# One core, 1 x 256 tokens: the gates of the first 128 tokens go through device memory by adding indirect DMAs, in both expert layers

## The chip, the cores and the metric

One core of one Trainium2 chip runs the whole program. The metric is device microseconds from start to end, lower is better. PE is the matrix engine (TensorE), DVE the vector engine (VectorE), ACT the scalar engine (ScalarE), POOL is GpSimd, and SP is the queue that issues most DMAs.

## The reference, cut to what matters

The reference is a block of two layers on 256 tokens of width 1024 (an attention-like mix, then an expert layer), followed by another block with its own attention and MLP. The change touches only the expert layer, which is computed twice (layer 0 and layer 1). Each has 16384 experts; an expert is one row of `u` and one row of `v`. Each of 8 heads chooses 16 experts per token, so a token has 128 (expert, gate) pairs, and the same expert may be chosen by more than one head:

```python
def block(args):
    ht, et, gt = args                       # tokens, their experts, their gates
    act = jax.nn.gelu(jnp.einsum('td,ted->te', ht, u[et]), approximate=False)
    return jnp.einsum('te,ted->td', gt * act, v[et])
```

## The kernel before

The expert layer (`peer`, L1282) does not gather. It computes the activation of every expert for every token and multiplies by a dense matrix of gates, which is zero where an expert is not chosen.

**First pass, U.** For j = 0 to 127, TensorE multiplies 128 experts' rows (U[j]) by all 256 tokens, GELU is applied, and the result lies in `av[:, j, 0:256]`: partition p and column j stand for expert 128 p + j. Each weight tile of 512 KB is split by ACT (`hi`) and DVE (`lo`) into two parts, two tiles ahead at most, and multiplied in three products (hi by hi, hi by lo, lo by hi). SP loads the raw tiles into a ring of four, each after `lo` of the tile four before it. From j = 80 to 125 (`PAIRED`) the hi products of both halves of the tokens' matrix run as one of 512 columns, and ACT and DVE add them together.

**Choices.** Meanwhile DVE works through `choices` (L1494), tile t = 0 (first 128 tokens) and then t = 1: the 16 greatest of each side, their sums, the greatest 16 of those, the experts' numbers (`EF`), then the exponentials on ACT (L1388) and the normalised gates (`GT`). A sum of costs (`COST`) spreads this over the steps up to j = 74.

**Products of one-hots.** At j = 76 and 77 PE transposes the experts' upper and lower numbers and the gates (`E1`, `E2`, `GT`), so that column n belongs to token n. From step `C_FROM` = 78 on, 64 groups of four tokens are worked off: for a token n, `oneA` holds the gate where iota equals the upper number, `oneB` is 1 where iota equals the lower, and PE multiplies the two, 128x128, which gives the token's gates for all 16384 experts in PSUM. POOL builds two of the four `oneA` of a group (L1353), ACT one or two in two steps (`hots_ac`, L1451), DVE the rest and `oneB` of all four (`hots`, L1572). A group may be built when the group two before it has been multiplied ("prod"). Groups are laid on steps by `GROUPS`; after group g, ACT copies the gates of later experts into `av` (L1405), DVE multiplies the earlier ones in place, and GELU results of the tokens done so far (`AHEAD`) go through `gtmp` and `gate_tile` (L1584). The one-hots lie in the memory of x, which is saved to `xs` in device memory ahead of the pass and read back in the second.

**Second pass, V.** For j = 0 to 127, ACT and DVE split `av[:, j, :]` (`coef_high`, L1466, `coef_low`, L1477) and the tile V[j], and PE adds twelve products of 512 columns into four banks. In layer 0 the same ring of four also carries 48 tiles of another weight (`ada`), which DVE multiplies on (`modulation_ve`, L1635).

Of the kernel before, what the change touches and what calls it, by code (L numbers as in the profile page):

```python
# [41 lines left out]
for _name, _w in [("ident", 128), ("ones", 128), ("bd64", 128), ("ntri", 128), ("nones", 128), ("sbm", 128), ("flip", 128),  # L42
                  ("fmask", 384), ("gm", 7 * 64), ("reset", 256), ("hot", 384), ("iota", 128), ("negrow", 8),
                  ("cneg", 2 * 16), ("cok", 2 * 16)]:
    CST[_name] = (_n, _n + _w)
    _n += _w
# [12 lines left out]
def constants():  # L59
# [40 lines left out]
    put("cneg", np.where(ok > 0, 0.0, NEG))  # L100
    return c
# [4 lines left out]
for _sem, _events in (  # L106
# [5 lines left out]
        ("cmp_pe", "cmp hidT kvc kc_ss lc PcTp")):  # L112
# [39 lines left out]
class Engine:  # L152
# [74 lines left out]

    def dma_start(self, out, in_):
        return Done(self, self.e and self.e.dma_start(out, in_), 16)
# [46 lines left out]
def declare(nc, arrays):  # L276
# [9 lines left out]
    io["xs"] = nc.dram_tensor("xs", (128, 2048), F32, kind="Internal").ap()  # L286
    return io
# [7 lines left out]
def build(nc, io, ctx):  # L295
# [967 lines left out]
    eT = [cbuf[:, 256 * i:256 * i + 256] for i in range(5)]  # L1263
# [8 lines left out]
    AFTER = [C_FROM + g * (C_TO - C_FROM) // 64 for g in range(64)]  # L1272
    GROUPS = [[g for g in range(64) if AFTER[g] == j] for j in range(128)]
    AHEAD = [4 * sum(AFTER[g] < j for g in range(64)) for j in range(128)]

# [6 lines left out]
    def peer(layer):  # L1282
# [21 lines left out]
        V = [table("v", 0)]  # L1304
        for j in range(128):
            if j < 127:
                V.append(table("v", j + 1))
            if layer == 0 and 4 <= j < 124 and (j - 4) % 2 == 0 and (j - 4) % 10 < 8:
# [12 lines left out]
        def peer_sp(sp):  # L1321
# [11 lines left out]
            sp.dma_start(io["xs"], xTf[:, :]).then_inc("x_out", layer)  # L1333
            for i, (src, freed, _) in enumerate(tiles):
                if i == 140:
                    sp.wait_ge("prod", layer, 63)
# [5 lines left out]
        gain = lambda c: P(f"f{layer}", c)  # L1342

        OWN = (0, 1, 2, 4, 5, 6)

        def peer_po(po):
            norm_po(po, k, gain)
            po.wait_ge("x_out", layer)
            for g in range(64):
                s = 4 * (g % 2)  # L1350
                po.wait_ge("eT", layer, g // 32)
                if g >= 2:
                    po.wait_ge("prod", layer, g - 2)  # L1353
                for i in range(2):
                    n = 4 * g + i
                    d = po.tensor_scalar(oneA[:, s + i, :], iota, eT[0][:, n:n + 1], EQ, eT[2][:, n:n + 1], MUL)
                d.then_inc("hotP", layer, g)

        def peer_ac(ac):
# [23 lines left out]
            for j in range(128):  # L1383
# [7 lines left out]
                if j in (C_FROM - 1, C_FROM):  # L1391
                    t = j - C_FROM + 1
                    ac.wait_ge("eTp", layer, t)
                    w = slice(128 * t, 128 * t + 128)
                    for i in range(3):
                        ac.activation(eT[i][:, w], PS[:, 4 + t, 128 * i:128 * i + 128], COPY)
                    for i in range(2):
                        d = ac.activation(eT[3 + i][:, w], PS[:, 4 + t, 128 * i:128 * i + 128], COPY, scale=-1.0)
                    d.then_inc("eT", layer, t)
                    if t == 0:  # L1400
                        ac.wait_ge("x_out", layer)
                        hots_ac(ac, 0)
                        hots_ac(ac, 1)
                for g in GROUPS[j - 1] if j else []:
                    ac.wait_ge("prod", layer, g)  # L1405
                    ac.activation(av[:, j:128, 4 * g:4 * g + 4], PS[:, 4 + g % 4, :].rearrange("p (t j) -> p j t", t=4)[:, j:128, :],
                                  COPY).then_inc("placed", layer, g)
                    if g < 62:
# [8 lines left out]
                elif j >= J_LATE:  # L1417
                    ac.wait_ge("eT", layer, 1)
# [22 lines left out]
        def gelu(ac, j, src):  # L1441
            n = AHEAD[j]
            if n:
                if j >= C_FROM + 3:
                    ac.wait_ge("gated", layer, "tile", j - 2)
                d = ac.activation(gtmp[:, j % 2, 0:n], src[:, 0:n], ACT.Gelu)
            if n < 256:
                d = ac.activation(av[:, j, n:256], src[:, n:256], ACT.Gelu)
            d.then_inc("gelu", layer, j)

        def hots_ac(ac, g):  # L1451
            s = 4 * (g % 2)
            ac.wait_ge("eT", layer, g // 32)
            for i in (2, 3) if g % 4 == 1 else (2,):
                n, a = 4 * g + i, oneA[:, s + i, :]
# [10 lines left out]
        def coef_high(ac, j):  # L1466
            if j >= 3:
                ac.wait_ge("wdone", V[j - 3])
            if j == 0:
                ac.wait_ge("hotP", layer, 63)  # L1470
                ac.wait_ge("hot", layer, 63)
                ac.wait_ge("gated", layer, 63)
# [21 lines left out]
        def choices(ve):  # L1494

            g, s = GT.rearrange("p (h k) -> p h k", h=16), SC.rearrange("p (h k) -> p h k", h=16)
            for t in range(2):
# [31 lines left out]
                if t:  # L1529
                    ve.tensor_tensor(g, s, s[:, :, 0:1].broadcast_to([128, 16, 16]), SUB).then_inc("gmax", layer)  # L1530
                hv = hot.rearrange("p (k c) -> p k c", k=16)
                for h in range(8):
# [10 lines left out]
                    yield 10  # L1543
            ve.wait_ge(*d)
            ve.wait_ge(*ve.tensor_copy(EI, EF).then_inc("dveC"))
            ve.tensor_scalar(E2.bitcast(U32), EI, 127, ALU.bitwise_and)
            ve.wait_ge(*ve.tensor_scalar(E1.bitcast(U32), EI, 7, ALU.logical_shift_right).then_inc("dveC"))
            ve.tensor_copy(E2, E2.bitcast(U32))
            ve.tensor_copy(E1, E1.bitcast(U32)).then_inc("e12", layer)
            yield 15  # L1550
            ve.wait_ge("gexp", layer)
            ve.wait_ge(*ve.tensor_reduce(st[:, 0:16], g, ADD).then_inc("dveC"))
            ve.wait_ge(*ve.reciprocal(st[:, 16:32], st[:, 0:16]).then_inc("dveC"))
            ve.tensor_tensor(g, g, st[:, 16:32].rearrange("p (h o) -> p h o", o=1).broadcast_to([128, 16, 16]), MUL).then_inc("gates", layer)
            yield 10

        COST = 2 * (16 * 15 + 6 + 28 + 8 * 13 + 8 * 30) + 25

        def peer_ve(ve):
# [12 lines left out]
            def hots(g):  # L1572
# [3 lines left out]
                ve.wait_ge("eT", layer, g // 32)  # L1576
                n = 4 * g + 3
                if g % 4 != 1:
                    ve.tensor_scalar(oneA[:, s + 3, :], iota, eT[0][:, n:n + 1], EQ, eT[2][:, n:n + 1], MUL)
                ve.tensor_tensor(oneB[:, s:s + 4, :], iota.rearrange("p (o e) -> p o e", o=1).broadcast_to([128, 4, 128]),  # L1580
                                 eT[1][:, 4 * g:4 * g + 4].rearrange("p (t o) -> p t o", o=1).broadcast_to([128, 4, 128]),
                                 EQ).then_inc("hot", layer, g)

            def gate_tile(j):  # L1584
                n = AHEAD[j]
                if n:
                    ve.wait_ge("gelu", layer, j)
                    ve.tensor_tensor(av[:, j, 0:n], av[:, j, 0:n], gtmp[:, j % 2, 0:n], MUL).then_inc("gated", layer, "tile", j)

            for j in range(128):  # L1590
                if j == C_FROM:
                    ve.wait_ge("x_out", layer)
                    hots(0)
# [7 lines left out]
                for g in GROUPS[j - 1] if j else []:  # L1601
                    ve.wait_ge("placed", layer, g)
                    ve.wait_ge("gelu", layer, j - 1)
                    m = av[:, 0:j, 4 * g:4 * g + 4]
                    ve.tensor_tensor(m, m, PS[:, 4 + g % 4, :].rearrange("p (t j) -> p j t", t=4)[:, 0:j, :], MUL).then_inc("gated", layer, g)
                    if g < 62:
# [81 lines left out]
        def peer_pe(pe):  # L1688
# [1431 lines left out]
```

## Time and profile before

| | us |
|---|---|
| median of 3 runs | 2362.92 |
| lowest, highest | 2362.66, 2363.53 |
| profiled execution, first to last instruction | 2361.0 |
| PE busy | 2335.1 (99%) |
| DVE busy | 1755.3 (74%) |
| ACT busy | 1367.7 (58%) |
| POOL busy | 463.4 (20%) |
| DMA, share of 16 engines | 54.6% |

The times of the rows are microseconds, where nothing else is said, and stand for one execution. A busy engine is one with an instruction in flight; PE's products overlap, so the distance between two starts says more than a duration. "x16" is a count, "<-" names what an idle engine waited for, and L170 and the like are lines of helpers, so that tiles and shapes tell the places apart.

### The profile page before, as it was taken

The page shows a single profiled execution, that of the slowest core. Times are in us where ns is not written, and L with a number is a line of the kernel's source. Part 1 is how long each engine was busy: PE and PEld are TensorE (multiplying, and loading weights), DVE is VectorE, ACT ScalarE, POOL GpSimd, SP SyncE. Part 2 cuts the span into 40 slices and gives each one's busy share as a digit, 9 for nine tenths or more (in the row PEclk, how much of TensorE's full clock was granted, in tenths as well). Part 3 has the DMA queues.
Part 4 walks back from the last instruction along what each step waited for, and adds up shares of the span by engine and source line. Part 5 has one row for each costly group of instructions (what it writes and reads, how often), then busy time and mean ns, then how long its engine had stood idle before and what let it go on. Part 6 is the DMA issues. An engine that isn't in the chain of part 4 may idle for free.

```text
span 2361.0 us, 40110 instructions
## 1 busy us (share of the span) xinstructions
PE 2335.1 (99%) x15655; PEld 2115.9 (90%) x15655; DVE 1755.3 (74%) x3335; ACT 1367.7 (58%) x2622; POOL 463.4 (20%) x411
## 2 busy tenths in 40 slices
PE   8999999999999999999999999999999999999999
PEld 8899999999888888888999999998888888899998
DVE  7967999788777777667599988885555555747864
ACT  6664445777655555566544467775554454666643
POOL 4720000788300000011000038870000000003000
PEclk9999999999999999999999999999999999999999
DMA  7234565444588888732266654446666675334452
GB/s 279 88 131 127 181 187 178 148 131 134 186 269 263 270 262 269 281 144 109 94 187 184 181 172 132 134 134 205 194 192 194 195 234 200 140 113 174 179 193 75
DMA packets 93283, 421.77 MB, mean 179 GB/s; under 512 B 10324, under 2 KB 12956, under 8 KB 85160
## 3 DMA queue, kind: packets, MB, share of 16 engines
q1 hardware_dynamic: 92784, 418.84, 54.6%
q8 instruction: 126, 2.06, 0.4%
q14 instruction: 61, 0.50, 0.1%
q10 hardware_dynamic: 312, 0.37, 0.0%
HBM read 415.98 MB, written 3.18 MB: 178 GB/s over the span
## 4 chain that ended last, share of the span: by engine, by line
PE 91%; DVE 6%; ACT 2%; DMA 1%; issue 1%; ACTq 0%; DVEq 0%
PE PS L170 90%; DVE r_sl L191 2%; DVE mem L191 1%; DVE mem L199 1%; ACT mem L181 1%; ACT r_sh L181 1%; DMA mem<-in_v 1%; PE PS L173 0%; DVE mem L205 0%; DVE mem L211 0%; DMA cst<-in_cst 0%; DVE r_gl L199 0%; DVE hT L199 0%; ACT L188 0%; DVE mem L195 0%
## 5 line engine op out<-in xcount | busy, mean ns | idle before, releaser
L191 DVE TENSOR_TENSOR r_sl<-mem,r_sh 128x1024 fp32r<-128x1024 f32 (+2 forms) x750 | 896.4, 1196 | 452.8 <-ACT r_sh L181 450.8
L181 ACT ACTIVATE r_sh<-mem 128x1024 fp32r<-128x1024 f32 (+2 forms) x750 | 767.5, 1024 | 493.9 <-PE PS L170 408.0
L170 PE MATMUL PS<-r_h,r_sh 128*128 128x256 f32 (+2 forms) x4800 | 752.6, 304 | 6.3 <-ACT r_h L181 2.8
L170 PEld LDWEIGHTS PS<-r_h,r_sh 128*128 128x128 f32 (+1 forms) x4800 | 647.5, 191 | 42.5 <-issue 8.9
L196 POOL TENSOR_SCALAR xT<-cst,mem 128x128 f32<-128x128 f32 x256 | 328.3, 1294 | 543.4 <-ACT mem L181 492.9
L170 PE MATMUL PS<-r_h,r_sl 128*128 128x256 f32 (+1 forms) x2832 | 400.7, 283 | 1.2 <-DVE r_sl L191 1.1
L170 PEld LDWEIGHTS PS<-r_h,r_sl 128*128 128x128 f32 (+1 forms) x2832 | 371.7, 191 | 10.9 <-DVE r_sl L191 2.2
L181 ACT ACTIVATE mem<-PS 128x256 f32<-128x256 f32 (+19 forms) x468 | 158.9, 351 | 324.1 <-PE PS L170 322.5
L170 PE MATMUL PS<-r_sh,r_ch 128*128 128x512 f32 x1024 | 276.1, 390 | 2.2 <-ACT r_sh L181 2.2
L170 PE MATMUL PS<-r_sh,r_cl 128*128 128x512 f32 x1024 | 274.8, 389 | 0.0
L170 PE MATMUL PS<-r_sl,r_ch 128*128 128x512 f32 x1024 | 274.7, 389 | 0.0
L170 PEld LDWEIGHTS PS<-r_sh,r_ch 128*128 128x128 f32 x1024 | 191.2, 188 | 47.0 <-ACT r_sh L181 4.9
L170 PEld LDWEIGHTS PS<-r_sh,r_cl 128*128 128x128 f32 x1024 | 192.2, 188 | 40.1
L170 PEld LDWEIGHTS PS<-r_sl,r_ch 128*128 128x128 f32 x1024 | 192.2, 188 | 40.0
L170 PE MATMUL PS<-xT 128*128 128x128 f32 x1024 | 130.0, 275 | 0.0
L170 PEld LDWEIGHTS PS<-xT 128*128 128x128 f32 x1024 | 122.8, 192 | 0.0
L191 DVE TENSOR_TENSOR r_cl<-mem,r_ch 128x256 fp32r<-128x256 f32 x256 | 106.9, 418 | 11.3 <-ACT r_ch L181 11.3
L181 ACT ACTIVATE r_ch<-mem 128x256 fp32r<-128x256 f32 x256 | 102.4, 400 | 3.9 <-issue 3.9
L181 ACT ACTIVATE mem<-mem 128x256 f32<-128x256 f32 (+5 forms) x153 | 79.8, 531 | 32.4 <-DVE mem L205 23.6
L170 PE MATMUL PS<-mem 64*15 64x64 f32 (+9 forms) x1014 | 96.4, 289 | 2.1 <-ACT mem L181 1.0
L170 PEld LDWEIGHTS PS<-mem 64*128 64x128 f32 (+4 forms) x1014 | 79.4, 153 | 20.9 <-issue 9.0
L181 ACT ACTIVATE small<-PS 128x256 f32<-128x256 f32 (+2 forms) x108 | 42.9, 398 | 78.3 <-PE PS L170 78.1
(170 smaller groups left out, 2504.4 us busy)
## 6 DMA issues: line engine op xcount, KB each, us to landing
mem<-in_u SPq DMA_DIRECT2D x256, 512.0 KB, 3.6
mem<-in_v SPq DMA_DIRECT2D x256, 512.0 KB, 4.4
mem<-in_w SPq DMA_DIRECT2D x16, 2048.0 KB, 8.2
mem<-in_ada SPq DMA_DIRECT2D x48, 512.0 KB, 4.9
mem<-in_in SPq DMA_DIRECT2D x9, 2048.0 KB, 8.8
mem<-in_wq SPq DMA_DIRECT2D x8, 2048.0 KB, 7.7
mem<-in_od_in SPq DMA_DIRECT2D x6, 2048.0 KB, 9.7
mem<-in_ev_in SPq DMA_DIRECT2D x5, 2048.0 KB, 14.4
```

What stands on the lines that cost most here:

```text
L170: return self.did(self.e and self.e.matmul(out, lhsT, rhs, start=start, stop=stop, skip_group_check=skip))
L181: return self.did(self.e and self.e.activation(out, in_, func, **kw))
L191: return self.did(self.e and self.e.tensor_tensor(out, a, b, op))
L196: return self.did(self.e and self.e.tensor_scalar(out, a, s1, s2, op0, op1))
L199: return self.did(self.e and self.e.scalar_tensor_tensor(out=out, in0=a, scalar=s, in1=b, op0=op0, op1=op1))
```

## The change

For the first 128 tokens of both layers the one-hots and their products are gone. Per layer:

- A buffer of 16384 x 128 numbers in device memory (`gd`, 8 MB) is written with zeros, by 16 DMAs from a part of x's memory that POOL has set to zero.
- The choices of tile 0 are finished early: exponentials at step 28, then gates (`GX`) and addresses (`IX` = expert x 128 + token).
- POOL issues 128 indirect DMAs that add: the n-th adds the n-th gate of each of 128 tokens (4 bytes each) at its address. It waits for completion after each 16 (one head). 48 are issued ahead of the first one-hot, then 3 after each group's.
- SP reads the buffer back in 32 blocks of 128 x 512 (four columns j by 128 tokens each), and DVE multiplies each into `av` (`gated_first`), the first at the end of the U pass, the others in the V pass at j = 1, 5, 9 and so on.
- The other 128 tokens have 32 groups in place of 64, over the same 48 steps. POOL builds one `oneA` per group, ACT one or two, DVE one or two. Their tokens lie at the end of `av`'s rows and are done in falling order.
- Some events of a later stage share a semaphore.

```diff
+    def scatter_add(self, out, index, in_):
+        at = bass.IndirectOffsetOnAxis(ap=index, axis=0)
+        return Done(self, self.e and self.e.indirect_dma_start(out, at, in_, None, compute_op=ADD), 16)
...
+    for layer in range(2):
+        io[f"gd{layer}"] = nc.dram_tensor(f"gd{layer}", (16384 * 128, 1), F32, kind="Internal").ap()
...
-    eT = [cbuf[:, 256 * i:256 * i + 256] for i in range(5)]
+    eT = [cbuf[:, 128 * i:128 * i + 128] for i in range(5)]
+    GX, IX = cbuf[:, 640:768], cbuf[:, 768:896].bitcast(U32)
+    gtile = [cbuf[:, 1024:1536]] + [hhi_raw_r[:, 512 * i:512 * i + 512] for i in range(3)]
...
-    AFTER = [C_FROM + g * (C_TO - C_FROM) // 64 for g in range(64)]
+    NG = 32
+    AFTER = [C_FROM + g * (C_TO - C_FROM) // NG for g in range(NG)]
...
+    FIRST_TOKEN = [124 - 4 * g for g in range(NG)]
+    ZEROED = 16
...
                 sp.wait_ge(*freed)
                 sp.dma_start(raw[i % 4], src).then_inc(f"raw{i % 4}", layer, i)
+                if 4 <= i < 4 + 2 * ZEROED and i % 2 == 0:
+                    sp.wait_ge("zero", "gd", layer)
+                    sp.dma_start(pieces_of_gd[(i - 4) // 2], xTf[:, 0:1024]).then_inc("gz", layer, (i - 4) // 2)
+                elif i == v_at[1]:
+                    sp.wait_ge("scat", layer, 127)
+                    gate_blocks(0)
+                elif i == v_at[3]:
+                    sp.wait_ge("wdone", U[127])
+                    for n in range(1, 4):
+                        gate_blocks(n)
+                elif i in v_at and i >= v_at[7] and (v_at.index(i) + 9) % 4 == 0 and (v_at.index(i) + 9) // 4 < 32:
+                    n = (v_at.index(i) + 9) // 4
+                    sp.wait_ge("gated", layer, "first", n - 3)
+                    gate_blocks(n)
...
             po.wait_ge("x_out", layer)
-            for g in range(64):
-                s = 4 * (g % 2)
-                po.wait_ge("eT", layer, g // 32)
+            po.memset(xTf[:, 0:1024], 0.0).then_inc("zero", "gd", layer)
...
+                po.wait_ge("gz", layer, ZEROED - 1)
+                po.wait_ge("gates", layer, 0)
+                for n in range(128):
+                    if n and n % 16 == 0:
+                        po.wait_ge("scat", layer, n - 1)
+                    po.scatter_add(io[f"gd{layer}"], IX[:, n:n + 1], GX[:, n:n + 1]).then_inc("scat", layer, n)
+                    yield
+
+            scatter = scattered()
+            for _ in range(48):
+                next(scatter)
+            for g in range(NG):
+                n = FIRST_TOKEN[g]
+                po.wait_ge("eT", layer)
                 if g >= 2:
                     po.wait_ge("prod", layer, g - 2)
-                for i in range(2):
-                    n = 4 * g + i
-                    d = po.tensor_scalar(oneA[:, s + i, :], iota, eT[0][:, n:n + 1], EQ, eT[2][:, n:n + 1], MUL)
-                d.then_inc("hotP", layer, g)
+                po.tensor_scalar(oneA[:, 4 * (g % 2), :], iota, eT[0][:, n:n + 1], EQ, eT[2][:, n:n + 1], MUL).then_inc("hotP", layer, g)
+                for _ in range(3):
+                    next(scatter, None)
...
-                if j == C_FROM - 8:
-                    ac.wait_ge("gmax", layer)
-                    ac.activation(GT, GT, ACT.Exp).then_inc("gexp", layer)
...
+                if j in (28, C_FROM - 8):
+                    t = int(j > 28)
+                    ac.wait_ge("gmax", layer, t)
+                    w = GT[:, 128 * t:128 * t + 128]
+                    ac.activation(w, w, ACT.Exp).then_inc("gexp", layer, t)
...
+            if j % 4 == 0:
+                ac.wait_ge("gated", layer, "first", j // 4)
             if AHEAD[j]:
                 ac.wait_ge("gated", layer, "tile", j)
             ac.activation(CH[j % 3][:, :], av[:, j, :], COPY).then_inc("c_hi", layer, j)
...
+                if t == 0:
+                    ve.wait_ge(*d)
+                    ve.wait_ge("col", 0)
+                    ve.wait_ge(*ve.tensor_scalar(half(E1, 0), half(EF, 0), 128.0, MUL, C("tok"), ADD).then_inc("dveC"))
+                    ve.wait_ge(*ve.tensor_copy(IX, half(E1, 0)).then_inc("dveC"))
+                    normalised(0, GX).then_inc("gates", layer, 0)
+                    yield 15
...
+            def gated_first(i):
+
+                ve.wait_ge("gelu", layer, 4 * i + 3)
+                ve.wait_ge(*gate_block_in(i))
+                w = av[:, 4 * i:4 * i + 4, 0:128]
+                ve.tensor_tensor(w, w, gtile[gslot(i)].rearrange("p (j t) -> p j t", j=4), MUL).then_inc("gated", layer, "first", i)
...
                 lo(ve, (U + V)[j + 1])
+                if j == 127:
+                    gated_first(0)
...
+                if j % 4 == 1 and j < 124:
+                    gated_first(j // 4 + 1)
...
-                if j in (C_FROM - 2, C_FROM - 1):
-                    t = j - C_FROM + 2
-                    w, b = slice(128 * t, 128 * t + 128), 4 + t
-                    bank_wait(pe, b)
+                if j == C_FROM - 2:
+                    bank_wait(pe, 4)
                     pe.wait_ge("e12", layer)
-                    pe.wait_ge("gates", layer)
+                    pe.wait_ge("gates", layer, 1)
```

## Rows read from the trace of the kernel before

**Rows 1.** Page, section 1: busy us, share of the span, instructions

```profile
PE 2335.1 (99%) x15655; PEld 2115.9 (90%) x15655; DVE 1755.3 (74%) x3335; ACT 1367.7 (58%) x2622; POOL 463.4 (20%) x411
```

**Rows 2.** Windows: span; busy PE, PEld, DVE, ACT, POOL; clock, DMA share, GB/s

```profile
178.00:425.00 247.00, 246.58 (x2058) 246.22 (x2057) 211.61 (x562) 120.58 (x185) 1.38 (x2) 1.00 0.57 168
425.00:621.80 196.80, 196.80 (x1341) 180.90 (x1340) 170.12 (x318) 150.09 (x420) 162.77 (x127) 1.00 0.44 134
621.80:975.00 353.20, 351.37 (x1554) 286.05 (x1553) 263.66 (x353) 182.13 (x269) 0.00 (x0) 1.00 0.82 270
...
1594.00:1943.00 349.00, 348.59 (x1540) 288.20 (x1539) 200.03 (x259) 176.75 (x259) 0.00 (x0) 1.00 0.67 203
```

**Rows 3.** Timeline of PE, layer 0: start us, us, instruction, count

```profile
198.54 2.17 PE L170 MATMUL PS<-r_h,r_sh 128*128 128x256 f32 x16 [0.29 <-ACT r_sh L181]
...
417.86 0.49 PE L173 MATMUL PS<-cst,mem 128*128 128x128 f32 x3
418.10 2.16 PE L170 MATMUL PS<-r_h,r_sh 128*128 128x256 f32 x16
...
427.15 1.95 PE L170 MATMUL PS<-xT 128*128 128x128 f32 x16
428.85 2.16 PE L170 MATMUL PS<-r_h,r_sh 128*128 128x256 f32 x16
...
431.81 1.06 PE L170 MATMUL PS<-xT 128*128 128x128 f32 x8
432.63 2.10 PE L170 MATMUL PS<-r_h,r_sh 128*128 128x512 f32 x8
...
435.51 1.06 PE L170 MATMUL PS<-xT 128*128 128x128 f32 x8
```

**Rows 4.** Groups by form, 424:616: count, busy us, mean ns, idle before

```profile
L191 DVE TENSOR_TENSOR xT<-cst,mem 128x512 f32<-128x512 f32 x64 | 43.9, 687 | 0.0
...
L196 POOL TENSOR_SCALAR xT<-cst,mem 128x128 f32<-128x128 f32 x128 | 164.1, 1294 | 271.7 <-ACT mem L181 246.5 <-PE PS L170 24.9
```

**Rows 5.** Timeline of DVE, layer 0, between the two tiles' choices

```profile
305.01 0.98 DVE L205 TENSOR_REDUCE mem<-mem 128x16 f32<-128x800 f32 x1
305.91 0.28 DVE L217 MAX8 mem<-mem 128x8 f32<-128x128 f32 x1
```

**Rows 6.** DMA issues: ns, first and last start; then KB, us to landing

```profile
L229 SPq DMA_DIRECT2D xs<-xT x2: 327/328/330, 169.4 to 1141.6; - x2
...
mem<-in_u SPq DMA_DIRECT2D x256, 512.0 KB, 3.6
...
out<-xT SPq DMA_DIRECT2D x8, 128.0 KB, 1.9
```

**Rows 7.** Instructions on tile xT, POOL's one-hots: ns min/median/max

```profile
L196 POOL TENSOR_SCALAR xT<-cst,mem x256: 784/1405/1858, 423.6 to 1584.1; 128x128 f32<-128x128 f32 x128
```

**Rows 8.** DMAs on tensor fd: ns, start us

```profile
L229 SPq DMA_DIRECT2D fd<-mem x1: 337/337/337, 1951.1 to 1951.1; - x1
L229 SPq DMA_DIRECT2D mem<-fd x1: 399/399/399, 1952.5 to 1952.5; - x1
```

**Rows 9.** Timeline of PE, layer 0, around step 70

```profile
405.03 1.12 PE L170 MATMUL PS<-r_h,r_sl 128*128 128x256 f32 x8
406.27 2.14 PE L170 MATMUL PS<-r_h,r_sh 128*128 128x256 f32 x16
```

**Rows 10.** ACT waits, second pass, layer 0, then 1: us, times, longest

```profile
ACT r_sh L181 <- DMA mem<-in_v: 82.1, 39, 3.7
...
ACT r_sh L181 <- PE PS L170: 169.6, 125, 1.6
```

**Rows 11.** Timelines of DVE and ACT, end of the first pass, layer 0

```profile
620.44 1.22 DVE L191 TENSOR_TENSOR r_sl<-mem,r_sh 128x1024 fp32r<-128x1024 f32 x1 [1.62 <-ACT r_sh L181]
...
620.31 0.41 ACT L181 ACTIVATE r_ch<-mem 128x256 fp32r<-128x256 f32 x1
```

**Rows 12.** Page, section 3: packets, MB, share of 16 engines

```profile
q1 hardware_dynamic: 92784, 418.84, 54.6%
```

More of the change, by code:

```diff
@@ L100, in constants @@
     put("cneg", np.where(ok > 0, 0.0, NEG))
+    put("tok", p)
     return c
@@ L1445, in gelu @@
                     ac.wait_ge("gated", layer, "tile", j - 2)
[L1446 to L1449, printed above, removed]
+                ac.activation(gtmp[:, j % 2, 0:n], src[:, 256 - n:256], ACT.Gelu)
+            ac.activation(av[:, j, 0:256 - n], src[:, 0:256 - n], ACT.Gelu).then_inc("gelu", layer, j)
         def hots_ac(ac, g):
             s = 4 * (g % 2)
-            ac.wait_ge("eT", layer, g // 32)
-            for i in (2, 3) if g % 4 == 1 else (2,):
-                n, a = 4 * g + i, oneA[:, s + i, :]
+            ac.wait_ge("eT", layer)
+            for i in (1,) if g % 2 else (1, 2):
+                n, a = FIRST_TOKEN[g] + i, oneA[:, s + i, :]
                 ac.wait_ge(*ac.activation(a, iota, ACT.Abs, bias=eT[3][:, n:n + 1]).then_inc("actC"))
@@ L1469, in coef_high @@
             if j == 0:
-                ac.wait_ge("hotP", layer, 63)
-                ac.wait_ge("hot", layer, 63)
-                ac.wait_ge("gated", layer, 63)
+                ac.wait_ge("hotP", layer, NG - 1)
+                ac.wait_ge("hot", layer, NG - 1)
+                ac.wait_ge("gated", layer, NG - 1)
+            if j % 4 == 0:
+                ac.wait_ge("gated", layer, "first", j // 4)
             if AHEAD[j]:
@@ L1494, in choices, with normalised @@
         def choices(ve):
-            g, s = GT.rearrange("p (h k) -> p h k", h=16), SC.rearrange("p (h k) -> p h k", h=16)
+            half = lambda a, t: a[:, 128 * t:128 * t + 128]
+            def normalised(t, out):
+                g = half(GT, t).rearrange("p (h k) -> p h k", h=8)
+                ve.wait_ge("gexp", layer, t)
+                ve.wait_ge(*ve.tensor_reduce(st[:, 0:8], g, ADD).then_inc("dveC"))
+                ve.wait_ge(*ve.reciprocal(st[:, 8:16], st[:, 0:8]).then_inc("dveC"))
+                return ve.tensor_tensor(out.rearrange("p (h k) -> p h k", h=8), g,
+                                        st[:, 8:16].rearrange("p (h o) -> p h o", o=1).broadcast_to([128, 8, 16]), MUL)
             for t in range(2):
@@ L1528, in choices @@
                 d = ve.tensor_copy(p16f, p16).then_inc("dveC")
-                if t:
-                    ve.tensor_tensor(g, s, s[:, :, 0:1].broadcast_to([128, 16, 16]), SUB).then_inc("gmax", layer)
+                g, s = (half(a, t).rearrange("p (h k) -> p h k", h=8) for a in (GT, SC))
+                ve.tensor_tensor(g, s, s[:, :, 0:1].broadcast_to([128, 8, 16]), SUB).then_inc("gmax", layer, t)
                 hv = hot.rearrange("p (k c) -> p k c", k=16)
@@ L1575, in hots @@
                     ve.wait_ge("prod", layer, g - 2)
[L1576 to L1579, printed above, removed]
+                ve.wait_ge("eT", layer)
+                first = FIRST_TOKEN[g]
+                for i in (2, 3) if g % 2 else (3,):
+                    n = first + i
+                    ve.tensor_scalar(oneA[:, s + i, :], iota, eT[0][:, n:n + 1], EQ, eT[2][:, n:n + 1], MUL)
                 ve.tensor_tensor(oneB[:, s:s + 4, :], iota.rearrange("p (o e) -> p o e", o=1).broadcast_to([128, 4, 128]),
-                                 eT[1][:, 4 * g:4 * g + 4].rearrange("p (t o) -> p t o", o=1).broadcast_to([128, 4, 128]),
+                                 eT[1][:, first:first + 4].rearrange("p (t o) -> p t o", o=1).broadcast_to([128, 4, 128]),
                                  EQ).then_inc("hot", layer, g)
@@ L1592, in peer_ve @@
                     ve.wait_ge("x_out", layer)
+                    ve.wait_ge("gz", layer, ZEROED - 1)
                     hots(0)
```

83 lines of the change are left out of this document (47 added, 36 removed).

## The prediction

> **What bounds the kernel now.** I read the page first: TensorE (PE) is busy in 2335.1 of the 2361.0 us of the profiled execution [rows 1]. Then the stages, through the table of windows [rows 2]. In layer 0 the plain part of the first pass (U[0] to about U[77]) runs from 198.5 [rows 3] to 424 us, the part with one-hot products from about 425 to 621.8, the second pass (V) from 621.8 to 975; layer 1 has the same stages some 972 us later. In the part with products PE is busy for all of its 196.8 us, while the other engines have room: DVE 170.1, ACT 150.1, POOL 162.8. So an instruction less on PE there is worth its whole time, as long as none of the others, or a transfer, becomes later than PE. The reader is to see that this holds in the second passes too [rows 2] (351.4 of 353.2, and 348.6 of 349), with the transfers at 0.82 of the DMA engines' time in layer 0 and 0.67 in layer 1.
>
> **What the edit takes from PE.** The products of one group (four tokens, eight records) stand between the blocks of two experts' rows. A single group starts at 431.81 and the next block at 432.63, 0.82 us; two groups start at 427.15 and the next block at 428.85, 1.70 us [rows 3]. Before, 64 groups lie on 48 steps: 16 steps with two and 32 with one, 16 x 1.70 + 32 x 0.82 = 53.4 us per layer. After, 32 groups lie one to a step: 32 x 0.82 = 26.2. That is 27.2 us less per layer, 54.4 in both. One set of three transposes goes (417.86 to 418.10 [rows 3]), 0.24 us per layer, 0.5 in both. Together 54.9 us, all on the path. Nothing else on PE changes.
>
> **What the edit takes from the others.** Per layer DVE loses 32 builds of 128x512 at 0.69 us [rows 4], 22 us, and half of its products with PSUM and of its per-tile products; POOL goes from 128 one-hots to 32; ACT loses half of its 160 two-step ones. None of these ends PE's wait now, so they are worth nothing by themselves. They pay for what is added.
>
> **The adding DMAs.** POOL issues 128 per layer, each with 128 elements of 4 bytes. The first gates and indices are there when DVE has ended the choices of the first tile: its last reduction runs at 305.01, and the first MAX8 of the second tile at 305.91 [rows 5]; three small operations more, about 308. POOL's first one-hot starts at 423.6 today [rows 6], so 48 issues have 115 us: up to about 2.3 us each with two completions in between. They are hidden by the plain part, in any case near the forecast. Then POOL has, for each group, one one-hot and three issues. The new length of that part is 48 steps of 2.88 us (a paired block, 432.63 to 435.51 [rows 3]) and 26.2 of products, 164.4 us, 5.14 us per group. POOL may fall behind by about 8 us before PE waits, since a one-hot is allowed from the end of the group two before it (9.5 us earlier, less its own 1.3).
> What one issue costs no row shows. The nearest below is SP's issue, 0.33 us, made by other means [rows 7]; the nearest on POOL itself is its one-hot: least 0.784, median 1.405, greatest 1.858 us [rows 6], mean 1.294 [rows 4]. I hold 0.33 and 1.86 as ends. I take 1.2: it is an operation of the same engine, and DVE, beside which the one-hots stretch from 0.78, will be less busy (by the losses above an estimated 125 of 164 us in place of 170 of 197). Then a group takes 3 x 1.2 + 1.29 = 4.9 of 5.14 us, and POOL is not late. The waits for completion, five of the eight in this part, last an estimated 2 us each: a small write to device memory was issued at 1951.1 and what waited for it at 1952.5, 1.4 us [rows 8]; 128 KB out took 1.9 [rows 7]. 10 us, less what the groups give back (27 x 0.25 = 6.7), stay within the 8. Cost taken: 0. The 128 are out after 27 groups, about step 118, before SP asks for them (at V[1]'s tile, step 125), so the wait put ahead of the loads ends at once.
> Of this the trace and the Trainium skill can be set side by side. The one-hot, which has one tensor input, took from 0.784 to 1.858 us beside a busy DVE [rows 6]. The Trainium skill (SBUF — State Buffer, section "SBUF: two separate sides") says that DVE and GpSimd lock a shared port pair for a whole instruction, and that descriptors for a GpSimd DMA can't be written while DVE runs a two-port operation. By that rule an issue would be stretched like the one-hot, and a mean of 1.4 us would make 2336 of the sum in place of 2313.
>
> **The zeroing.** One memset of 128x1024 on POOL (nothing else is queued there then) and 16 writes of 512 KB on SP's queue between U tiles 4 and 34. SP waits for the memset at tile 4, which it issues only after DVE has split U[0], past 198.5 us; the copy of x that the memset waits for was issued at 169.4 [rows 7]. The transfers stand at 0.57 of their time there [rows 2], 1.65 us of each 2.88 us step; one more tile in every second step makes 0.85. A U tile lands 3.6 us after issue [rows 7]; with a write ahead of it some 1.7 later, 5.3. Its place in the ring comes free four steps ahead of need, 11.5 us, less about 3 for the splits: 8.5. Cost 0; without this cover it would be 16 x 1.7 = 27 us per layer.
>
> **Exponentials in two halves.** ACT changes tables at step 28 too. The existing change at step 70 moved the next block from 405.99 (405.03 and eight records of 0.12) to 406.27 [rows 9], 0.28 us. Two layers: +0.6.
>
> **Reading back.** 32 transfers of 256 KB per layer. At 270 GB/s for 0.82 of the time [rows 2], 256 KB take 0.8 us of the engines. Layer 1 has room (0.67, and none of ACT's waits there names a V tile [rows 10]). In layer 0 ACT already waits for V tiles 39 times, 82.1 us [rows 10]; that costs PE only what separates 353.2 - 351.4 from nothing, about 1.8 us, because ACT stands about 1.5 us ahead. 28 of the transfers come in steady state: nothing below, 28 x 0.8 = 22 us above. I take 3, nearer to the lower end, as ACT's present waits show how much of such lateness is swallowed. DVE gets 32 products of 128x512 at about 0.69 [rows 4], 22 us; it has 264 of 353 busy in layer 0 [rows 2]: 0. The first one stands, on DVE, behind the split of V[0] (620.44 + 1.22) and ahead of ACT's first coefficient copy, which is at 620.31 now [rows 11], before PE needs it at 621.8. With 0.69 for the product and 0.41 for the copy it is ready at 622.8, 1.0 late. Queued behind it on ACT are the last GELU, a table load and the split of V[1], for which PE waits a little today, so that this lateness isn't added twice. 0 to 1.5 us per layer, I take 0.8: +1.6. Blocks 1 to 3 wait for U[127]; they are needed some 6 us later: 0.
>
> **The sum** against the profiled execution: 2361.0 - 54.9 + 0.6 + 1.6 + 3 = 2311.3. The median of the runs is 1.9 above the span (2362.9): 2313.2, say 2313. The lower end, with nothing for reading back and the junction, is 2308.6; 2306 allows another 0.1% for the difference between executions.
>
> **Rivals.**
> 1. POOL becomes the bound. PE waits for hotP as soon as three issues and a one-hot exceed 5.14 us plus the slack: 27 x (3s + 1.29 - 5.14) + 10 - 8.3 us per layer. It begins at s = 1.26, is worth 11.6 us per layer at 1.405 (2336 in total), meets the gain (27) at s = 1.60, and at 1.858 is 48 per layer: 2313 + 97 = 2410. For it: POOL's own median of 1.405, and eight completions in line. Against it: the least of 0.784, and a DVE freed of a quarter of its work. This is the rival on the other side; it decides from 1.6 us. Beside it a page's rule: the Trainium skill (DMA: Bandwidth & Descriptors, section "Latency and other measured facts") gives about 1 us to a GpSimd DMA's first byte; by that price, as an estimate, the sum stays 2313.
> 2. The elements crowd the DMA engines. Each engine gets 8 of a DMA's 128. Queue 1 takes 0.546 x 16 x 2361 us for 92784 packets, 222 ns each, for 4.5 KB [rows 12]. In the part with products the engines are free for 0.56 of 5.14 us, 2.9 us per group, or 120 ns per element. At 222 ns they would be short by 3 x 8 x 0.222 - 2.9 = 2.4 us per group, 66 per layer, and U tiles late: 2313 + 130 = 2443. For it: an add reads and writes its target. Against it: 4 bytes are not 4.5 KB.
> 3. Layer 0's V tiles come late by the full 22 us: 2332. Speaking for it are ACT's 39 waits; against it, the little that they cost now.
>
> **How the numbers follow.** Forecast (2306 to 2325): 0.50. Rival 1 mild, s between 1.3 and 1.57, 2325 to 2358: 0.08; rival 3: 0.06; all these are faster. Rival 1 at its point of balance: 0.06. Rival 1 beyond it: 0.22; rival 2: 0.08; both slower. A difference of 0.2% (4.7 us) is about what a measurement of this kernel tells from none. Faster 0.64, same 0.06, slower 0.30. The range goes from 2306 to the upper end of an issue's price, 2410; rival 2 and a little of 1 stay out, 0.12 in all. The likeliest case's own range is 2306 to 2325.
>
> **What would show it.** Right: in the part with products, groups of eight records with no gap ahead of them and steps of 2.88 us; that part 165 us long in place of 197; POOL with gaps that end on PE; the plain part's 247 us unchanged within 1. Wrong: PE idle ahead of products with POOL as releaser (rival 1), ACT's splits waiting for in_u (rival 2) or longer for in_v (rival 3); an issue on POOL over 1.6 us; SP standing at V[1] for the last of the 128.

## The result, and the profile after

The changed kernel takes 2440.38 us (median of 4 runs, 2439.89 to 2443.02), the kernel before 2363.23 (2362.66 to 2364.31): 1.0325 times as long, 95% interval 1.031 to 1.0339. The prediction was 2313, with 2410 as upper end. The forecast was a faster kernel; it is a slower one, outside the range. In the profiled executions the span goes from 2361.0 to 2438.4 us, 77.4 more.

The page after, sections 1 to 3, answering to [rows 1] and [rows 12]: busy time; the granted clock over the span in tenths; the queues.

```profile
PE 2323.6 (95%) x15137; PEld 2089.6 (86%) x15137; DVE 1723.0 (71%) x3283; ACT 1322.3 (54%) x2430; POOL 674.8 (28%) x477
...
PEclk9999999898999999999999999899999999999999
...
q0 software_dynamic: 36864, 0.15, 4.0%
```

PE has 518 instructions less than in [rows 1] and is busy for 11.5 us less, but the span has grown: PE now stands idle for 115 us, where it stood for 26. The windows of layer 0 say where, in the columns of [rows 2]: plain first pass, part with products, second pass.

```profile
180.00:427.00 247.00, 246.67 (x2056) 246.13 (x2055) 212.03 (x569) 123.56 (x189) 95.36 (x49) 1.00 0.72 202
427.00:660.20 233.20, 189.66 (x1079) 167.38 (x1077) 135.39 (x255) 123.80 (x321) 173.86 (x111) 0.91 0.51 114
660.20:1017.00 356.80, 353.41 (x1552) 285.86 (x1553) 280.84 (x383) 183.38 (x270) 0.00 (x0) 1.00 0.86 290
```

Nearly all of it is in the middle line (233.2 in place of 196.8). There PE is busy for 189.7 of 233.2 us at a granted clock of 0.91, while no engine looks full: POOL, the busiest after PE, has 174. The timelines show what a busy share can't. First PE (start, us, instruction, count, idle before it), answering to the groups in [rows 3]:

```profile
428.59 1.06 PE L173 MATMUL PS<-xT 128*128 128x128 f32 x8
429.40 2.16 PE L173 MATMUL PS<-r_h,r_sh 128*128 128x256 f32 x16
431.39 1.12 PE L173 MATMUL PS<-r_h,r_sl 128*128 128x256 f32 x8
434.33 1.62 PE L173 MATMUL PS<-xT 128*128 128x128 f32 x8 [1.82 <-issue]
...
442.48 1.05 PE L173 MATMUL PS<-xT 128*128 128x128 f32 x8
443.29 2.09 PE L173 MATMUL PS<-r_h,r_sh 128*128 128x512 f32 x8
445.22 1.11 PE L173 MATMUL PS<-r_h,r_sl 128*128 128x256 f32 x8
449.73 2.05 PE L173 MATMUL PS<-xT 128*128 128x128 f32 x8 [3.40 <-issue]
451.43 3.76 PE L173 MATMUL PS<-r_h,r_sh 128*128 128x512 f32 x8
```

The group alone takes the 0.8 us that the prediction gave it (428.59 to 429.40), but PE pauses ahead of 20 of the 32 groups, 42.5 us in all. Then POOL in the same stretch:

```profile
438.83 1.56 POOL L233 DMA_INDIRECT gd<-mem  x1 [0.30 <-issue]
439.86 1.39 POOL L199 TENSOR_SCALAR xT<-cst,mem 128x128 f32<-128x128 f32 x1
441.44 2.52 POOL L233 DMA_INDIRECT gd<-mem  x1 [0.18 <-issue]
444.27 2.42 POOL L233 DMA_INDIRECT gd<-mem  x1 [0.30 <-issue]
446.99 1.54 POOL L233 DMA_INDIRECT gd<-mem  x1 [0.30 <-issue]
448.00 1.63 POOL L199 TENSOR_SCALAR xT<-cst,mem 128x128 f32<-128x128 f32 x1
449.81 1.60 POOL L233 DMA_INDIRECT gd<-mem  x1 [0.17 <-issue]
```

This is a chain without a hole: POOL always has the next instruction at hand. The one-hot of the group at 449.73 ends at 449.63 (448.00 + 1.63), right ahead of it; it had three issues in front of it, and each occupies POOL for 1.54 to 2.52 us and then for another 0.30 in which nothing is counted as busy. Of the 59 us of the 233 in which POOL isn't busy, 23 are such steps and 10 are waits for completion; from 427 to 628 us it waits for nothing else. The rest comes after the last issue. The one-hot's record begins before the issue ahead of it has ended (448.00 against 446.99 + 1.54 = 448.53), so what it adds is less than its 1.63. The Trainium skill (Perfetto Trace Analysis, section "GPSIMD Engine Instruction") says to time GpSimd by the distance from start to start and not by the reported duration; this trace agrees, as the mean of 1.63 us below is 1.22 once the overlap is taken off. POOL's groups of the part with products (count, busy, mean ns, idle before), answering to [rows 4]:

```profile
L233 POOL DMA_INDIRECT gd<-mem x80 | 137.3, 1716 | 32.6 <-issue 22.6 <-DMA gd<-mem 10.1
L199 POOL TENSOR_SCALAR xT<-cst,mem 128x128 f32<-128x128 f32 x32 | 52.0, 1628 | 9.9 <-PE PS L173 8.5 <-ACT mem L184 1.5
```

From 427.19, where the 49th issue starts, to 628.17, where the last one ends, POOL needs 201 us for 26 rounds of three issues and a one-hot, and two issues more: 80 issues x 1.716 = 137; the steps between them 23; completions 9; 26 one-hots x 1.23 = 32. The 26 rounds alone end at 624.71 (the start of the last issue but one): 7.60 us per round, where the part had 5.14 to give. All of the 8.5 us for which POOL's one-hots wait for PE lie after 628.

### The profile page after: what moved, and what is told of

It reads as the page before. It is cut to its first block, busy times and chain, and to the rows that moved or that the text cites. A ratio compares the mean times of both kernels' runs of the same rounds, so it can differ in the third digit from the quotient of the medians.

```text
span 2438.4 us, 38826 instructions
## 1 busy us (share of the span) xinstructions
PE 2323.6 (95%) x15137; PEld 2089.6 (86%) x15137; DVE 1723.0 (71%) x3283; ACT 1322.3 (54%) x2430; POOL 674.8 (28%) x477
## 3 DMA queue, kind: packets, MB, share of 16 engines
q0 software_dynamic: 36864, 0.15, 4.0%
q8 instruction: 121, 1.98, 0.3%
## 4 chain that ended last, share of the span: by engine, by line
PE 82%; DVE 8%; issue 5%; ACT 3%; DMA 2%; ACTq 0%; DVEq 0%
PE PS L173 82%; DVE r_sl L194 2%; DMA mem<-in_v 2%; ACT r_sh L184 2%; DVE mem L194 2%; DVE mem L202 1%; ACT mem L184 1%; DVE hT L202 0%; PE PS L176 0%; DVE mem L208 0%; DVE xT L194 0%; DVE mem L214 0%; DVE xT L199 0%; DMA cst<-in_cst 0%; DVE r_gl L202 0%
## 5 line engine op out<-in xcount | busy, mean ns | idle before, releaser
L173 PE MATMUL PS<-r_h,r_sh 128*128 128x256 f32 (+2 forms) x4800 | 771.5, 309 | 6.6 <-ACT r_h L184 2.8
L173 PEld LDWEIGHTS PS<-r_h,r_sh 128*128 128x128 f32 (+1 forms) x4800 | 663.7, 194 | 47.6 <-issue 9.1
L233 POOL DMA_INDIRECT gd<-mem x256 | 461.7, 1804 | 365.0 <-DVE mem L194 259.6
L184 ACT ACTIVATE mem<-PS 128x256 f32<-128x256 f32 (+13 forms) x398 | 143.5, 371 | 392.7 <-PE PS L173 383.4
L173 PE MATMUL PS<-xT 128*128 128x128 f32 x512 | 82.7, 312 | 85.7 <-issue 69.9
L173 PEld LDWEIGHTS PS<-xT 128*128 128x128 f32 x512 | 72.7, 219 | 92.9 <-issue 72.6
L194 POOL TENSOR_TENSOR hT<-xT,small 128x256 f32<-128x256 f32 x6 | 5.9, 988 | 384.8 <-ACT small L184 384.8
L199 POOL TENSOR_SCALAR xT<-cst,mem 128x128 f32<-128x128 f32 x64 | 104.8, 1642 | 19.9 <-PE PS L173 16.9
```

The lines of the kernel that those rows point to most:

```text
L173: return self.did(self.e and self.e.matmul(out, lhsT, rhs, start=start, stop=stop, skip_group_check=skip))
L184: return self.did(self.e and self.e.activation(out, in_, func, **kw))
L194: return self.did(self.e and self.e.tensor_tensor(out, a, b, op))
L199: return self.did(self.e and self.e.tensor_scalar(out, a, s1, s2, op0, op1))
L233: return Done(self, self.e and self.e.indirect_dma_start(out, at, in_, None, compute_op=ADD), 16)
```

## The experiments

### What one issue costs: `m1_issue`

A program of its own, with nothing of the layers in it: POOL issues indirect DMAs of 4-byte elements in phases of 16, and DVE is idle or runs one kind of operation beside it.

```diff
+        # phases: (partitions, add, what DVE does)
+        phases = [(128, True, None), (128, True, "tt"), (128, True, "ts"), (128, True, "pt"), (64, True, None), (128, False, None), (16, True, None)]
...
+                for n in range(N):
+                    col = N * k + n
+                    at = bass.IndirectOffsetOnAxis(ap=ix[0:p, col:col + 1], axis=0)
+                    kw = {"compute_op": ALU.add} if add else {}
+                    e.indirect_dma_start(io["gd"], at, gx[0:p, col:col + 1], None, **kw).then_inc(sc, 16)
```

> A program of its own, which leaves out the whole computation: POOL issues 16 indirect DMAs in a row in each of seven phases; adding with 128 partitions and DVE idle, beside DVE adding two tensors in SBUF (128x1024), beside DVE multiplying one tensor in SBUF by a number, beside DVE adding a tensor in PSUM to one in SBUF, then with DVE idle again adding with 64 partitions, plainly writing with 128, adding with 16. In the changed kernel an issue took 1.54 us at least, 1.80 in the mean. Theory A (the price is GpSimd's own work, stretched by DVE): 1.54 us with DVE idle, 0.3 or so between two, and 2.2 to 2.6 beside the two-tensor addition. Theory B (the price is all DVE's lock): under 1.0 with DVE idle. If the work is by elements, 64 partitions take about 0.8 and 16 about 0.2; if it is by instruction, all take 1.5. A plain write shows whether adding costs POOL anything: I expect no.

One line each from POOL's timeline: 128 partitions with DVE idle, with DVE adding two tensors of SBUF, with DVE scaling one tensor, with DVE adding PSUM and SBUF; 64 partitions; 128 plain writes; 16 partitions.

```profile
12.36 1.54 POOL L73 DMA_INDIRECT gd<-gx,ix  x1 [0.30 <-issue]
...
47.47 2.21 POOL L73 DMA_INDIRECT gd<-gx,ix  x1 [0.30 <-issue]
...
94.92 1.88 POOL L73 DMA_INDIRECT gd<-gx,ix  x1 [0.30 <-issue]
...
129.80 1.54 POOL L73 DMA_INDIRECT gd<-gx,ix  x1 [0.30 <-issue]
...
162.28 1.42 POOL L73 DMA_INDIRECT gd<-gx,ix  x1 [0.30 <-issue]
...
192.92 0.97 POOL L73 DMA_INDIRECT gd<-gx,ix  x1 [0.31 <-issue]
...
214.27 1.29 POOL L73 DMA_INDIRECT gd<-gx,ix  x1 [0.30 <-issue]
```

With nothing beside it, an adding issue is busy for 1.54 us and costs POOL 1.85 us from start to start, as theory A had it; that adding would cost POOL nothing was wrong (1.54 against 0.97 for a plain write). So the price that the prediction took (1.2) wasn't to be had at all, and the balance that it had worked out for rival 1 (1.60) is passed without any contention. DVE adds to it: 2.52 from start to start beside additions of two tensors, 2.18 beside one-tensor operations, nothing beside one that reads PSUM. The Trainium skill (SBUF — State Buffer, section "SBUF: two separate sides") names as the operations of DVE that lock the shared pair those in a two-port mode and, against a GpSimd instruction that reads SBUF, those with two inputs in SBUF. The trace agrees in which operations slow an issue, though not in how much: the loss (0.67 beside an operation of 1.23 us) is smaller than a whole operation. That the scaling runs in a two-port mode, and that an issue reads SBUF, no row shows.

### The rest of the sum: `e1_first48`

Only the issues ahead of the first one-hot are left, so that POOL is free in the part with products.

```diff
-                    sp.wait_ge("scat", layer, 127)
+                    sp.wait_ge("scat", layer, 47)
...
-                for n in range(128):
+                for n in range(48):
```

> The changed kernel with only the first 48 of the 128 adding DMAs per layer (the gates of the other 80 choices of the first 128 tokens are left out), SP waits for the 48th. Theory (POOL's queue: one-hots stand behind issues that take 2.1 us each): the part with products shrinks from 231.7 us to 165 to 168, the whole to 2310 to 2318 us. Rival (elements crowd the DMA engines, or the read back, the zeroing and the early exponentials cost more than counted): 2335 or more. If the clock after PE's pauses is what cost, it goes with them and can't be told apart here.

2308.7 us in one run, with 2363.8 for the kernel before on that chip; span 2306.9. Its part with products and the junction:

```profile
427.00:594.00 167.00, 166.25 (x1067) 150.29 (x1066) 131.84 (x252) 120.07 (x316) 24.00 (x30) 1.00 0.50 157
...
594.34 1.17 PE L173 MATMUL PS<-r_sh,r_ch 128*128 128x512 f32 x4 [1.09 <-ACT r_ch L184]
```

From the first product at 427.17 to the second pass at 594.34 it is 167.2 us, where it was 194.6 (427.15 [rows 3] to 621.8 [rows 2]): 27.4 gained (the prediction: 27.2, less 0.8 for the junction). So the products' worth, the zeroing, the reading back and the junction were right, and the whole miss lies in the 80 issues per layer. Whether it is POOL's time, their elements or the clock behind PE's pauses this run can't tell, as all three go with them. Without issues between them POOL's one-hots take 0.80 us each here (24.00 for 30).

### Taking POOL's one-hots from behind the issues: `e2_hots_dve`

DVE builds POOL's one-hot too; POOL issues all 128 in a row.

```diff
-            for _ in range(48):
-                next(scatter)
-            for g in range(NG):
...
+            for _ in scatter:
+                pass
...
-                for i in (2, 3) if g % 2 else (3,):
+                for i in (0, 2, 3) if g % 2 else (0, 3):
```

> The changed kernel, POOL's one-hot of each group built by DVE, POOL issues its 128 in one sequence. Theory: PE no longer waits for POOL inside the part with products; 80 issues at 2.1 us and 5 completions at 2.7 from 424 on end near 606, with read-back near 612, 15 to 20 us after PE could start on V: 2313 + 2 x 15 = 2335 to 2350 us, faster than before by about 1%. Rival (the DMA engines or DVE's lock are the cause, not the order on POOL): PE's pauses inside the part stay and the time stays above 2400.

2340.35 us (2333.53 to 2342.13), 0.9896 of before (0.9876 to 0.9916). No pause is left in the part with products; one of 12.6 us stands behind it. POOL, SP's first block, DVE and PE there:

```profile
598.43 1.55 POOL L233 DMA_INDIRECT gd<-mem  x1 [0.30 <-issue]
...
L236 SPq DMA_DIRECT2D mem<-gd x2: 326/326/327, 601.5 to 1563.6; - x2
...
604.48 0.69 DVE L194 TENSOR_TENSOR mem<-mem 128x512 f32<-128x512 f32 x1 [11.48 <-DMA mem<-gd]
...
605.82 2.05 PE L173 MATMUL PS<-r_sh,r_ch 128*128 128x512 f32 x4 [12.63 <-ACT r_ch L184]
```

With 2 x 12.6 of waiting taken off 2340 it would be some 2315, an estimate. All the adding DMAs and their elements are still there, in the same stage, and the pauses are gone. The cause is therefore POOL's queue, and it has two faces: the one-hots in line behind the issues (after), and the last issue later than the first pass (here, 598.4 against a pass that ends at 593).

### Fewer per group, more ahead: `e3_64_2`

```diff
-            for _ in range(48):
+            for _ in range(64):
...
-                for _ in range(3):
+                for _ in range(2):
```

> The changed kernel with 64 issues ahead of the first one-hot and 2 after each, in place of 48 and 3. Theory: POOL's total work from the first gates on is what counts (128 x 2.1 + 7 x 2.7 + 32 x 1.2 = 326 us from 309 on, then the read back), so the first groups are 25 to 35 us late but nothing is behind afterwards: V starts near 642 in place of 660 in each layer, 2395 to 2410 us in all. Rival (each group's period alone counts, and lateness ahead of the first is added to it): 27 groups save 2.1 us, 57, and lose 34 ahead, which gives about the same; if instead the first one-hots' lateness is the worse, over 2440.

2409.25 us in one run (before: 2363.8), within what was expected. The 64th issue starts at 458.24, and the first product waits for the one-hot behind it:

```profile
458.24 1.55 POOL L233 DMA_INDIRECT gd<-mem  x1 [0.30 <-issue]
459.27 1.37 POOL L199 TENSOR_SCALAR xT<-cst,mem 128x128 f32<-128x128 f32 x1
...
460.75 2.05 PE L173 MATMUL PS<-xT 128*128 128x128 f32 x8 [33.14 <-issue]
```

The 48 ahead were near the most that fit: the last of them ends at 423.83 in the changed kernel. What isn't issued ahead is paid between the groups, and the other way round; this order of the queue moves the wait and removes 31 of the 132 us that separate the changed kernel from e1.

### A cheaper issue in the same place: `e5_plain`

```diff
-        return Done(self, self.e and self.e.indirect_dma_start(out, at, in_, None, compute_op=ADD), 16)
+        return Done(self, self.e and self.e.indirect_dma_start(out, at, in_, None), 16)
```

> The changed kernel with plain writes in place of adding ones, all else as it is (where two heads of a token chose the same expert, the sum of their gates is left out, the later write stays). A plain issue took 0.97 us in place of 1.54 with DVE idle. Theory (the price of an issue on POOL, times three, plus a one-hot, against 5.14 us per group): with 1.23 and 0.30 between two a group takes 5.7 us, 27 x 0.55 + 10 - 8 = 17 us late per layer, 2335 to 2360 us in all, against 2440. Rival (order or pauses cost, whatever an issue takes): above 2400.

2357.72 us in one run, with 2364.43 for the kernel before on that chip. Number, form, queue and waits are those of the changed kernel; the sum of two gates at one element is left out. What differs is the price (and what the DMA does at its target, where e2 kept the adding ones and lost the pauses):

```profile
L233 POOL DMA_INDIRECT gd<-mem x256 | 295.2, 1153 | 362.3 <-DVE mem L194 259.6 <-issue 74.5 <-DMA gd<-mem 28.2
```

1.15 us in place of the 1.80 of the changed kernel brings the time from 2440 to 2358: it follows the price of an issue, as rival 1 says. In the part with products these issues are busy for a mean of 1.20 us, just what the prediction took, and still the time is 49 us above e1's:

```profile
L233 POOL DMA_INDIRECT gd<-mem x80 | 96.0, 1200 | 32.1 <-issue 22.6 <-DMA gd<-mem 9.5
```

The round there is 3 x (1.20 + 0.26) + 1.12 = 5.5 us against 5.14, and three completions take 2.9 to 3.3 us each. An issue that is busy for 1.2 us would thus have missed 2313 as well, by the 0.26 between two and by the waits.

### Starting earlier: `e7_early` and `e8_early_pool`

In e7, on top of e2, the gates are normalised and the addresses of the first two heads made before the experts' numbers of the other six are done, the exponentials move from step 28 to 24, and the zeroing ends by tile 18 (eight of its writes at once behind U[3]).

```diff
-                if 4 <= i < 4 + 2 * ZEROED and i % 2 == 0:
+                if i == 3 or 4 <= i < 20 and i % 2 == 0:
...
-                po.wait_ge("gates", layer, 0)
                 for n in range(128):
+                    if n in (0, 32):
+                        po.wait_ge("gates", layer, 0, 1 if n == 0 else 7)
...
-                if j in (28, C_FROM - 8):
+                if j in (24, C_FROM - 8):
...
+                    if t == 0 and h in (1, 7):
+                        w = slice(0, 32) if h == 1 else slice(32, 128)
...
+                        ve.tensor_copy(IX[:, w], E1[:, w]).then_inc("gates", layer, 0, h)
```

> As the kernel with DVE's one-hots, and the chain of issues starts earlier: gates are normalised once head 1 of the first 128 tokens is through (step 25 in place of 36; exponentials at step 24), indices of heads 0 and 1 go first, the others when they are there, and the zeroing is done by about tile 18 (eight pieces while the first tiles wait, then eight beside U tiles). Theory: POOL's chain of about 290 us ends near 570, before V at about 594, PE waits neither inside nor at the end: 2308 to 2316 us, 2.1 to 2.3% faster than before. Rival (a further cost shows once this wait is gone: DVE full, or eight zero writes in a row ahead of tile 4): 2320 to 2335.

2310.05 us (2309.07 to 2314.15), 0.9772 of before (0.9755 to 0.9788): faster than both kernels. POOL's first and last issue, the part with products, and the junction:

```profile
279.70 1.88 POOL L233 DMA_INDIRECT gd<-mem  x1 [99.75 <-DVE mem L205]
...
577.83 1.55 POOL L233 DMA_INDIRECT gd<-mem  x1 [0.30 <-issue]
...
424.00:594.00 170.00, 170.00 (x1100) 154.29 (x1100) 141.84 (x288) 125.33 (x328) 119.07 (x69) 1.00 0.66 158
...
596.00 1.17 PE L173 MATMUL PS<-r_sh,r_ch 128*128 128x512 f32 x4 [1.07 <-ACT r_ch L184]
```

All 128 issues with their seven completions take 299.7 us in a row (279.70 to 579.38). They end 17 us ahead of the second pass, and PE is busy for all of the 170 us; DVE has room for the 32 one-hots more (142 of 170).

e8 is e7 with the one-hot back on POOL, 64 issues ahead and two per group:

```diff
+            for _ in range(64):
+                next(scatter)
+            for g in range(NG):
...
+                for _ in range(2):
+                    next(scatter, None)
```

> As the kernel with early gates, but one one-hot of each group stays on POOL, with 64 issues ahead of the first and 2 after each. Theory (what matters is POOL's total from the first gates on): 128 x 2.1 + 7 x 2.7 + 32 x 1.2 = 326 us from 277 on, end near 600, V a few us late, groups at 5.3 against 5.14: 2315 to 2335 us. If one-hots on POOL beside issues are themselves the trouble, whatever the total: over 2350.

2356.98 us in one run, 22 above the upper end of what was expected. PE and POOL at the first groups:

```profile
434.84 2.05 PE L173 MATMUL PS<-xT 128*128 128x128 f32 x8 [7.43 <-issue]
...
437.53 1.56 POOL L233 DMA_INDIRECT gd<-mem  x1 [0.30 <-issue]
438.56 1.39 POOL L199 TENSOR_SCALAR xT<-cst,mem 128x128 f32<-128x128 f32 x1
440.12 1.60 POOL L233 DMA_INDIRECT gd<-mem  x1 [0.18 <-issue]
442.02 2.31 POOL L233 DMA_INDIRECT gd<-mem  x1 [0.30 <-issue]
443.79 1.54 POOL L199 TENSOR_SCALAR xT<-cst,mem 128x128 f32<-128x128 f32 x1
```

POOL's whole line explains it: 128 issues x 1.90, 0.27 between them, seven completions of 15.4 us together, and 32 one-hots x 1.14, make 330 of the 335.4 us from 278.10 to 613.55. From the first issue to the last group at the old pace there are 306 (278 to 584 in e1), so PE gets behind by about the rest; the second pass starts at 620.78, 26.4 later than e1's. The one-hots' 36 us per layer are what e7 gives to DVE, and that decides between 2357 and 2310. The expectation had counted 326 us from 277 on and yet put the second pass "a few us late"; by its own count the line ended at 603 and the last one-hot two issues ahead of that, near 599, some 15 us behind the 584 of e1, and the line was 9 us longer than that. The time lies where the expectation had put its rival (one-hots beside issues are the trouble whatever the total, over 2350); against that rival speaks only this sum, which leaves it nothing to explain.

## Why the prediction was wrong, point by point

The prediction has two groups of rows exchanged: what it takes of POOL's one-hots from [rows 6] stands in [rows 7], and what it takes of SP's issues and landings from [rows 7] stands in [rows 6]. The numbers are those of the rows.

- *PE bounds every stage, and what it loses counts in full.* Right. e1 and e7 show 167.2 us for the part (596.00 - 428.85 in e7); 164.4 was the sum for the groups and blocks up to step 125.
- *The price of one adding issue, s = 1.2, between 0.33 and 1.86.* This step failed. It occupies POOL for 1.96 us in the plain part and 1.72 in the part with products, and for 0.26 more until the next instruction: 1.98 in the formula, outside the range. The 0.26 that was left out decides that: 1.72 alone gives 37 us per layer, 2387 in all. The one-hot was the wrong neighbour to measure it by: an issue's price is made of 0.97 for a plain write, 0.57 for the adding and 0.30 between two, and a one-hot shows none of them. The argument that a less busy DVE would bring it down was about contention (0 to 0.67 us), where most of the price is fixed. The rule of the Trainium skill on the shared ports (SBUF — State Buffer, section "SBUF: two separate sides") had been worked out to a mean of 1.4 and 2336; its direction was right, and it too lacked the fixed part.
- *The one-hot, 1.29, and the completions, 2 each.* Right: 1.22 net of overlap, and 10.1 us for five. (POOL waits for seven per layer and not eight; the eighth is SP's.)
- *POOL may lag by 8 us before PE waits.* Wrong, the second mis-sized term. There is such slack only where POOL runs ahead, and here it never does. POOL's first one-hot ends at 426.4 and three issues stand before the second; the second group is already 2 us late (434.33, where e1's distance of 3.77 gives 432.36).
- *Rival 1, 27 x (3s + 1.29 - 5.14) + 10 - 8.3.* The right mechanism, in the right place. With s = 1.98 it gives 58 us per layer, and without the cushion of 8.3 it gives 66; the second pass starts 64.5 us later than in e1, after the 1.4 us by which its first pass starts later are taken off. The chance of 0.22 behind its balance was too small because the price's range ended, at both sides, at rows of other operations.
- *48 issues ahead fit into 115 us, up to 2.3 each.* Right, and barely: 309.53 to 423.83.
- *Zeroing costs 0; changing tables 0.3 per layer.* From U[0] to the first product it is 228.42 us after and 228.61 before, so neither shows. e7's eight writes at once change nothing either (228.41).
- *Reading back 3 in layer 0, the junction 0.8 per layer.* The second pass of layer 0 grows from 352.4 to 355.8, 3.4; layer 1's by nothing (346.2 before, 345.8 after). PE waits 1.09 at the junction. ACT's waits for V tiles went from 82.1 to 98.0 us [rows 10], shown under this list; 16 us more of ACT's waiting cost PE 3.
- *Rival 2, elements that crowd the DMA engines.* False: queue 0 has 4.0% of 16 engines' 2438 us for 36864 packets, 42 ns each and not 222.
- *Rival 3.* False, by the 3.4 us above.
- The account of the 77.4 us: parts with products +37.1 and +36.4; second pass of layer 0 +3.4; U[0] starts 1.6 later; the rest together -1.1. Why U[0] starts between 198.5 and 200.4 in one kernel or another wasn't found.
- The clock, which the prediction left out: after the pause of 3.40 us the granted clock is 0.50, the lower of the two levels (1.2 GHz in place of 2.4), until the first block behind it is through; eight products take 2.05 us in place of 1.06, the block 3.56 in place of 1.93. The same follows other pauses of that length, in full or in part (0.50 from 595.9 to 601, 0.67 from 511.9 to 516), but not the one ahead of the group at 617.22 (1.00 from 617 to 622). It makes the stage's 0.91. It is hardly a loss on top: POOL sets the pace and doesn't wait for PE up to 628, and behind that the clock is 1.00. That is read from the trace; no run changed the clock alone.

The rows named above: POOL's issues ahead of the first one-hot (305:424), ACT's waits in the second pass of layer 0, and the windows right behind the pause (span, PE's busy time, clock, DMA share, GB/s).

```profile
L233 POOL DMA_INDIRECT gd<-mem x48 | 94.3, 1964 | 149.9 <-DVE mem L194 129.8 <-issue 13.7 <-DMA gd<-mem 6.3
...
ACT r_sh L184 <- DMA mem<-in_v: 98.0, 53, 4.1
...
449.70:455.00 5.30, 5.27 (x17) 0.50 0.46 99
455.00:463.00 8.00, 7.72 (x49) 0.98 0.42 70
```

What stays open: with POOL's one-hots on DVE, how much a POOL without waits for completion would give. These waits (15 to 20 us per layer) keep two heads' additions to one element apart; whether the sums come out right without them wasn't tried.

## What to carry to other kernels

When a change puts a new kind of instruction on an engine's queue, its price from start to start is worth a measurement of its own, as the nearest row of another operation bounds it neither above nor below; what counts is the whole line on that queue up to its last consumer, gaps and completions included. Slack is credited only to an engine that the trace shows running ahead. And an operation that PE waits for (here a one-hot of 0.8 us) doesn't belong behind a slow queue of work that nobody waits for yet: given to an engine with room (e2), the same DMAs turned from +3.3% into -1.0%, and started earlier as well (e7) into -2.3%.

## What the hardware showed beyond that

- The time that an adding indirect DMA keeps POOL busy depends little on its number of elements: 1.29 us for 16 partitions, 1.42 for 64, 1.54 for 128; adding in place of writing costs 0.57.
- Waiting for the completion of the last of 16 takes 1.2 to 1.6 us in the idle program, and up to 4.6 in the kernels, where the DMA engines also carry weights.
- A busy share hides a queue that is full: POOL was the bound of a stage at 174 of 233 us, with up to 0.30 us after each issue that counts as busy nowhere.
